# Expert weight chunks of a mixture-of-experts stage: the order of fixed and variable steps on TensorE, the place of a phase's products, and a nine to six split of the copies

## What is computed

```python
logits = einsum('nd,de->ne', xf, w_router)            # 256 tokens, 8 experts
top_logits, top_idx = lax.top_k(logits, 2)            # each token goes to 2 experts
gates = softmax(top_logits, axis=-1)
def expert_block(xb, e):                              # rows of one expert
    h = silu(xb @ w1[e]) * (xb @ w3[e])               # 1024 -> 3584, twice
    return h @ w2[e]                                  # 3584 -> 1024
out = zeros.at[tok].add(y * gate)                     # back to the tokens
```

## Time and profile before

| | |
|---|---|
| median of three runs | 3204.41 us (3202.76 to 3207.50) |
| the profiled execution | 3191.41 us, span of its instructions 3189.6 us |
| PE / DVE / ACT busy | 91% / 49% / 33% of the span |
| mean granted clock of TensorE | 0.960 of full speed |
| expert chunks 2 to 83 | from the issue at 829.41 us to the last landing at 1905.8 us |

### The profile page before, as it was taken

How to read it: one execution, slowest core, us unless ns; L and a number is a source line. 1 busy time by engine, 2 the same in 40 slices (tenths; PEclk the granted TensorE clock), 3 DMA queues, 4 the chain that set the end, 5 groups by cost and what they waited for, 6 DMA issues and landing times.

```text
span 3189.6 us, 67930 instructions
## 1 busy us (share of the span) xinstructions
PE 2887.9 (91%) x26308; PEld 1876.5 (59%) x26308; DVE 1565.4 (49%) x5142; ACT 1042.2 (33%) x2749; POOL 0.2 (0%) x4
## 2 busy tenths in 40 slices
PE   8979999978888888888888887989999999899998
PEld 7858887856455555555555545444444444556887
DVE  5641005563567676777676673784322210454331
ACT  3121002221455545554555552253211100243210
POOL 0000000000000000000000000000000000000000
PEclk9979999988999999999999998999999999999999
DMA  5444434454599999999999981100121221211441
GB/s 206 167 172 171 146 133 158 151 207 159 191 327 322 326 321 325 327 327 315 329 318 330 322 306 65 58 26 27 66 77 69 79 79 66 79 54 54 154 150 66
DMA packets 205858, 576.06 MB, mean 181 GB/s; under 512 B 6496, under 2 KB 6624, under 8 KB 179040
## 3 DMA queue, kind: packets, MB, share of 16 engines
q1 hardware_dynamic: 205536, 571.72, 52.0%
HBM read 570.65 MB, written 1.05 MB: 179 GB/s over the span
## 4 chain that ended last, share of the span: by engine, by line
PE 60%; DMA 21%; DVE 13%; issue 3%; ACT 2%; DVEq 1%; SPq 1%; ACTq 0%
PE P L497 43%; DMA ring<-ws_moe 20%; PE P L913 4%; DVE arena L1860 4%; DVE ring L1860 2%; PE P L686 1%; PE P L544 1%; PE P L608 1%; DVE small L1518 1%; PE P L618 1%; DVEq L1857 1%; PE P L627 1%; PE P L881 1%; PE P L576 1%; PE P L958 1%
## 5 line engine op out<-in xcount | busy, mean ns | idle before, releaser
L497 PE MATMUL P<-arena,ring 128*128 128x256 f32 (+1 forms) x2784 | 900.2, 484 | 24.7 <-ACT arena L1157 24.7
L497 PEld LDWEIGHTS P<-arena,ring 128*128 128x128 f32 x2784 | 531.9, 192 | 383.0 <-issue 335.4
L913 PE MATMUL P<-arena 128*32 128x256 f32 x6496 | 368.4, 379 | 12.1 <-DVE rstd L1833 6.6
L913 PE MATMUL P<-ring,arena 128*32 128x256 f32 x4256 | 279.3, 414 | 80.0 <-DMA ring<-ws_moe 71.2
L497 PE MATMUL P<-X_sb,ring 128*128 128x256 f32 x1504 | 333.7, 383 | 2.9 <-ACT X_sb L1136 1.6
L497 PEld LDWEIGHTS P<-X_sb,ring 128*128 128x128 f32 x1504 | 286.6, 192 | 45.1 <-issue 3.1
L1860 DVE COPY arena<-ring 128x256 f32 x1120 | 234.6, 290 | 146.8 <-DMA ring<-ws_moe 134.6
L913 PEld LDWEIGHTS P<-arena 128*32 128x32 f32 x6496 | 213.3, 110 | 150.4 <-DVE ring L1860 9.1
L1860 DVE COPY arena<-arena 128x256 f32 x1120 | 233.7, 290 | 74.1 <-DMA arena<-ws_moe 63.3
L913 PEld LDWEIGHTS P<-ring,arena 128*32 128x32 f32 x4256 | 148.3, 119 | 196.5 <-DMA ring<-ws_moe 83.7
L1351 ACT ACTIVATE arena<-ring 128x256 f32 x560 | 181.5, 405 | 222.5 <-DMA ring<-ws_moe 163.6
(11 more groups left out here) (360 smaller groups left out, 2564.7 us busy)
## 6 DMA issues: line engine op xcount, KB each, us to landing
ring<-ws_moe SPq DMA_DIRECT2D x84, 2048.0 KB, 13.8
arena<-ws_moe SPq DMA_DIRECT2D x84, 2048.0 KB, 15.5
ring<-ws_b SPq DMA_DIRECT2D x137, 1024.0 KB, 4.8
ring<-ws_a SPq DMA_DIRECT2D x67, 1024.0 KB, 4.9
cst_sb<-cst SPq DMA_DIRECT2D x1, 1664.0 KB, 8.5
X_sb<-xT SPq DMA_DIRECT2D x1, 1024.0 KB, 4.8
X_sb<-ctxT SPq DMA_DIRECT2D x1, 1024.0 KB, 4.9
out<-Y SPq DMA_DIRECT2D x2, 512.0 KB, 2.6
```

The lines of the kernel that those rows point to most:

```text
L497: ins = nc.tensor.matmul(bank(i, n), blockap(s, b % SLOT), rhs(kk), start=kk == 0, stop=kk == k - 1)
L913: ins = nc.tensor.matmul(acc(g // 2)[BR * j:BR * (j + 1), g % 2], x[:, b * BR:(b + 1) * BR], weights_of(b), start=k == 0, stop=last and kk ...
```

## The change

It does three things and leaves all data and all arithmetic as they are.

PE: of a chunk's fixed steps only the first three stand ahead; the variable step kk = 0 follows, then the fixed step 3 (which now carries the signal `fixed_done` or `rows_done`), then the variable steps 1 to 3.

ACT and DVE: the work on banks 1 and 2 of a phase that ended moves from ahead of copy step 2 to ahead of copy step 1. For the `flips_first` chunk all three banks are done ahead of the wait for the chunk, and ACT's `store_flip` moves to ahead of copy step 1.

NDVE goes from 10 to 9: DVE makes nine copies in each step, ACT six.

```diff
-NDVE = 10
+NDVE = 9
 ...
-                        for kk in range(CK):
+
+                        def fixed(kk):
                             for g in range(2):
                                 ins = rows_by(g, kk, lambda b: w4[:, b, :, kk])
-                        ins.then_inc(sem("rows_done" if last else "fixed_done"), 1)
+                            return ins
+
+                        for kk in range(CK - 1):
+                            fixed(kk)
                         for kk in range(CK):
+                            if kk == 1:
+                                fixed(CK - 1).then_inc(sem("rows_done" if last else "fixed_done"), 1)
                             u = CK * c + kk
                             pe.wait_ge(sem("copied_dve"), u + 1)
                             pe.wait_ge(sem("copied_act"), u + 1)
 ...
                         if ended:
-                            silu(ph - 1, 0)
+                            for b in range(NB if flips_first(c) else 1):
+                                silu(ph - 1, b)
                         act.wait_ge(sem(f"moe_w{c % 2}"), 32 * (c // 2 + 1))
                         for kk in range(CK):
                             u = CK * c + kk
-                            if kk == 2 and ended:
-                                silu(ph - 1, 1)
-                                silu(ph - 1, 2)
+                            if kk == 1 and ended:
                                 if flips_first(c):
                                     store_flip(up_index(ph - 1))
+                                else:
+                                    silu(ph - 1, 1)
+                                    silu(ph - 1, 2)
 ...
                         if ended:
-                            take_rows(ph - 1, 0)
+                            for b in range(NB if flips_first(c) else 1):
+                                take_rows(ph - 1, b)
                         dve.wait_ge(sem(f"moe_w{c % 2}"), 32 * (c // 2 + 1))
                         for kk in range(CK):
                             u = CK * c + kk
-                            if kk == 2 and ended:
+                            if kk == 1 and ended and not flips_first(c):
                                 take_rows(ph - 1, 1)
                                 take_rows(ph - 1, 2)
```

## The result

The changed kernel took 3176.75 us (four runs, 3171.39 to 3178.65) beside 3203.59 (four runs) for the kernel before, a ratio of 0.9910 (95% interval 0.9895 to 0.9925). A second set, five runs of the changed kernel and 23 of the kernel before, gave 0.9909 (0.9895 to 0.9922). That is 27 us less by the first pair of medians and 29 by the ratios. Forecast were 3174 us and 30 less.

A forecast was written before the change was run, and what follows sets the result against it. The prediction took the one-buffer `ring` loop of load and copies as the bound: 23.7 us from loops, 1.4 at start and 4.8 at end make 29.9, giving 3174 from the 3204.41 median, range 3161 to 3194.

The forecast's parts named there:

- What bounds the kernel: Expert stage: the one-buffer `ring` loop of load, four copy steps, next load sets the pace, 26.08 us per two chunks.
- The work in a ring chunk: Landing to next issue: 8.90 or 9.34 becomes 8.52 us behind an up phase, 9.44 becomes 8.63 behind a down phase.
- The new wait of DVE for `silu`: Ring chunk behind an up phase: DVE's moved products wait some 0.4 us for ACT's first `silu`, delaying all later copies.
- The load keeps its length, less 15%: `ring` loads: 15% of the 27.9 us loop gain given back, leaving 23.7 us; load stays 16.5 to 16.9.
- the last of my signs of being wrong: `ring` loop: the forecast is wrong if the load answers to the pace; no size given.
- Rival (a): DMA engines full, load grows by what copies give up; only start and end gain, 6.2 us, 3198; chance 0.12.
- Rival (b): Nothing given back, earlier arena landings help ring loads: about 0.87 us a loop, 40 us total, 3164; chance 0.09.
- Rival (d): Longer `silu` wait, other gains covered: each loop gives half of 0.72 us, 3184; chance counted within the forecast's spread.
- The 13 us between the profiled execution and the median: Profiled execution 3191.41 us against median 3204.41: the prediction said this difference lies in no term of its sum.
- Start: Before the issue at 829.41 us: one fewer expert number loaded and shorter copies bring the issue 1.4 us sooner.
- End: Chunk 80: products done ahead of its landing let PE start sooner; chunk 82 issued 3.9 to 5.6 us sooner, 4.8 taken.
- ACT as the bound (c): Copies: a sixth ACT copy costs 0.403 us, a step 2.42, so the kernel is slower, 3234 us; chance 0.05.

The follow-up runs named there:

- loads by half: Changed kernel with 16 KB runs, plus each DMA holding two steps, reloaded when these are done, work starting on a landed half: 2998.65 us, 0.9390 of the kernel before.

## Why the prediction was right, and where it was not

**What bounds the kernel**: right. The loop of one buffer set the pace: taking copies out shortened it, with PE's work the same.

**The work in a ring chunk**: right. 8.51 for 8.52 behind an up phase, 8.63 for 8.63 behind a down phase, mean saving 0.72 in the first pair of traces and 0.76 in both, for 0.72. The new wait of DVE for `silu` was 0.32 for 0.4. PE's signal was never last in a ring chunk, as costed. That the last copies wait for nothing holds in all ring chunks of the two traces but the two named above.

**The load keeps its length, less 15%**: wrong, and this is the step that failed. I took 15% given back from one fast stretch of 65 us; over the whole range of the experiments it is 45%. In the mean of the two pairs of traces the loops kept 16.6 us, where 23.7 were forecast. So the loop came to 25.91 and 25.76 us and not to 25.4 or 25.5, the load to 17.2 and 17.1 and not to 16.5 to 16.9, and the last of my signs of being wrong, that the load answers to the pace, came true. Why it answers stays open. Rival (a) holds by about half. Rival (b) falls: the loop gained 0.42 us and not 0.87. Rival (d) had nearly the right gain for a loop, 0.36, but not for its reason, since the wait for `silu` was shorter than forecast.

**The 13 us between the profiled execution and the median** do lie in a term of the sum: the second trace of the kernel before took 3209.2 us, 18 more than the first, and 14 of them are in its 39 loops, nearly all in the load. My forecast took the load of a quick execution for that of the kernel.

**Start**: 1.8 us for 1.4. **End**: 3.6 for 4.8. I took the middle between PE at full and at half clock, and in both traces its first three steps ran at about half clock (0.53 and 0.55 granted), after 4.5 us of idle time.

**ACT as the bound (c)**: fell. Six copies start within 1.86 us of the first one's start and the `silu` (1227.86 to 1229.72, ACT's start being 0.02 ahead of DVE's), 0.31 each. At the full length of an instruction, 0.403 us, it would have been 2.42.

**The sum** came out at 27 to 29 for 30. The loops lacked 7 us. In their place stand 1.7 us ahead of the first expert load and behind the last one, which no term had, and 3 to 5 us that no section shows. The method was right in mechanism but for the load, and lucky in size.

## What to carry to other kernels

Where a buffer is loaded again as soon as its work is done, cost an edit in the loop of that buffer, landing to issue to landing, and ask what is late next: here the order on PE alone gave nothing and nine to six alone 10 us, and the whole change 29. Measure how the load answers to the pace before counting on the gain, by a kernel that leaves most of the work out. And look at the run length of the loads first: in the kernel before, the same bytes in runs of 16 KB took 4.2% off the launch, and the whole reordering of the engines 0.9%.

## What the runs showed of the hardware

Loads of 2 MB in runs of 2 KB moved 324 to 346 GB/s at a DMA share of 0.98 to 1.02, in runs of 16 KB 373 at 0.94, and 393 to 395 at 0.98 to 0.99 with loads by half. So a share near 1 meant two quite different rates: divided by the share it is 330 to 339 GB/s with 2 KB and 395 to 401 with 16 KB. The Trainium skill says (Perfetto Trace Analysis, DMA Optimizations) that going from 2 KB to 4 or 8 KB can improve throughput dramatically. The runs agree in direction, with 327 GB/s in the changed kernel at 2 KB and 373 at 16 KB, 14% more; 4 and 8 KB were not run.

The same kernel's load in this stage differed by 0.33 us in the mean between two executions (16.62 and 16.95), 14 us in its loops. One profile of a kernel bound by loads does not give a term of that size.
